# Both heads' causal masks of a peak block issued one behind the other

## The chip, the cores and the metric

The kernel runs on one core of one Trainium2 chip. The time is the device time of one execution, in microseconds (us), as the median of several runs. TensorE is PE in the profile, and its weight loads are PEld; VectorE is DVE, ScalarE is ACT, GpSimd is POOL, and SyncE is SP.

## The reference

One inference step of a two-layer trunk: a chunked gMLP layer, then a forgetting-attention layer with 16 heads of width 64, over a prompt of 1024 positions and 8 decoded samples. The part that matters here is the attention of the prompt (abridged):

```python
logits = jnp.einsum('nqhd,nkhd->nhqk', q, k).astype(jnp.float32) * (FA_HEAD_DIM ** -0.5)
decay = jnp.swapaxes(c_q, 1, 2)[..., :, None] - jnp.swapaxes(c_k, 1, 2)[..., None, :]
causal = k_pos[None, :] <= q_pos[:, None]
logits = jnp.where(causal, logits + decay, -jnp.inf)
p = jax.nn.softmax(logits, axis=-1)
return jnp.einsum('nhqk,nkhd->nqhd', p.astype(v.dtype), v)
```

A softmax wants the largest logit of each query row before its exponentials. All heads are computed, and all products are f32 in effect: the large ones are three passes over a split of both operands into a high and a low part.

## The kernel before, in words

The gMLP layer fills the first 990 us or so. The attention layer follows in eight phases `phase(j)`, each for one pair of heads, j = 0 to 7; phases 1 to 6 are one hardware loop. Phases 0 to 6 last 81.7 us each. In each of them TensorE, in an order written out by hand, does two things by turns:

- `step(j + 1, q, n)`: 64 pieces of three 512-column matmuls (the helper `three`, L1669 to L1671) that project keys, queries, values and gates of the next pair of heads. `steps(a, b)` issues pieces a to b.
- the attention of the pair j: `peak`, `spread`, `scores` and `values`.

Phase 7 has no next pair. Its `steps` are empty, and what stood between the attention's parts is gone.

`peak(j, qt)` finds the largest logit for the 128 queries of block qt, for both heads. For each head TensorE multiplies the queries with the keys 0 to (qt + 1) * 128 (L1944: one matmul for qt 0 to 3, two for qt 4 to 7, the second with 128, 256, 384 or 512 columns; f32 with 4-byte weights). Then it adds the causal mask to the last 128 columns by a matmul of a bf16 mask with a bf16 identity (L1945), which signals `m_done` once per head. DVE's `peak` waits for `m_done` of a head, then reduces that head's block to one number a row (L1381, one custom instruction and a read of its accumulator into `nmin`) and signals `nl_ready`.

The blocks live in PSUM. For qt under 4, both heads of a block share a pair of banks, and two pairs alternate. For qt from 4, head 0 always has `pair(2)` and head 1 `pair(1)`. So head h of block qt can be written only when DVE has reduced head h of block qt - 1, and TensorE waits for it on `nl_ready`:

```python
if qt == 4:
    pe.wait_ge(S("nl_ready"), 16 * j + 8) if h == 0 else pe.wait_ge(S("mb_ready"), 2 * j + 1)
if qt > 4:
    pe.wait_ge(S("nl_ready"), 16 * j + 2 * qt + h - 1)
```

For qt 4, head 1 waits for `mb_ready`: `spread(j, 0)` (L1955) has put the first half's row numbers into `pair(1)`, and ACT's `shift` copies them out (L888). `peak_round` on DVE rounds the numbers of four blocks (L1387) ahead of each `spread`. After block 7, `scores(j, 0)` (L1974, L1975) writes to head 1's pair and waits for DVE's last reduction. From the scores the work goes to DVE (`exponents`, L1420), ACT (`probs`, L897 and L899), POOL (`p_low`, L524) and back to TensorE (`values`, L1993 to L1995).

In phases 0 to 6, blocks 0 and 1 stand together behind six pieces of steps, blocks 2 and 3 together behind three more, and each of the blocks 4 to 7 has three or four pieces between itself and what comes next. In phase 7 the blocks 4 to 7 and `scores(7, 0)` follow one another with nothing between. After phase 7's first scores, POOL sends for the samples' queries (`load_q`, tile `qb`), DVE scores the paged cache (L1364, L1367) between its other work, and the output projection and the sample's tail end the kernel.

Of the kernel before, what the change touches and what calls it, by code (L numbers as in the profile page):

```python
# [59 lines left out]
def wait(eng, sem, value):  # L60

    if isinstance(value, int) and value <= 0:
        return
    eng.wait_ge(sem, value)
# [7 lines left out]
def trunk(nc, units, w_ada0, w_ada, c_t, x_t, cols_d, ws_t, bs_row, ln_rows, table, cache_k, cache_v, cache_f,  # L72
          y_out, ys_out, k_out, v_out, f_out, kqv_s_out, vn_out):
    ctx = ExitStack()
    with ctx:
        sems = {}

        def S(name):
            if name not in sems:
                sems[name] = ctx.enter_context(nc.semaphore(name))  # L80
            return sems[name]
# [14 lines left out]
        def const(name, shape, dt=F32):  # L96
            n = 1
            for s in shape[1:]:
                n *= s
            t = at(name, shape, dt, const_end[0])  # L100
            const_end[0] += (n * (2 if dt == BF16 else 4) + 31) // 32 * 32
            assert const_end[0] <= 229368
            return t
# [88 lines left out]
        identb = const("identb", [P, P], BF16)  # L192
        ones = const("ones", [P, P])
        maskb = const("maskb", [P, P], BF16)
# [69 lines left out]
        def pair(n):  # L264
            return ps[n][:, :, :].rearrange("p a b -> p (a b)")
# [14 lines left out]
        def peak_out(qt, h):  # L280

            return ps[1 + qt % 2][:, h, 0:(qt + 1) * P] if qt < 4 else pair(2 - h)[:, 0:(qt + 1) * P]
# [1381 lines left out]
        def _(pe):  # L1664
            mm = nc.tensor.matmul
# [260 lines left out]
            def peak(j, qt):  # L1926

                qs = slice(qt * P, (qt + 1) * P)
                if qt == 0:
                    pe.wait_ge(S("kq_lo"), 4 * j + 4)  # L1930
                    wait(pe, S("arg_ready"), 24 * j)
                if qt == 1:
                    pe.wait_ge(S("v_hl"), j + 1)
                if 2 <= qt < 4:
                    pe.wait_ge(S("nl_ready"), 16 * j + 2 * qt - 2)
                for h in range(2):
# [4 lines that stand above are left out]
                    out = peak_out(qt, h)  # L1941
                    for k in range(0, (qt + 1) * P, HALF):
                        ks = slice(k, min(k + HALF, (qt + 1) * P))
                        mm(out[:, ks], QA[:, h, qs], KA[:, h, ks], start=True, stop=ks.stop < (qt + 1) * P)  # L1944
                    mm(out[:, qs], maskb[:, :], identb[:, :], start=False, stop=True).then_inc(S("m_done"), 1)  # L1945

            def spread(j, half):

# [68 lines left out]
            def phase(j, more):  # L2017
# [5 lines left out]

                steps(0, 6)
                peak(j, 0)
                peak(j, 1)
                if not more:
                    pe.wait_ge(S("ev_s"), 4 * KB)
                    pe.wait_ge(S("zs_done"), 4 * KB)
                    turn(1, 0)  # L2030
                steps(6, 9)
                peak(j, 2)
                peak(j, 3)
                steps(9, 13)
# [56 lines left out]
            for b in range(KB):  # L2091
# [18 lines left out]
                if b == 6:  # L2110
# [7 lines left out]
                    for c in range(2):  # L2118
                        last = mm(bank(6)[:, c:c + 1], ex[:, c, :, :].rearrange("p b h -> p (b h)"), ones[0:NS, 0:1],
                                  start=True, stop=True)  # L2120
# [19 lines left out]
            for n in range(NS):  # L2140
                s, (odd, p) = n % 4, divmod(n, NP)
                pe.wait_ge(S(f"pages_in{s}"), 16 * NP * (n // 4 + (5 if s < 2 else 1)))
                for h in range(2):
                    for g in range(4):
                        rows = slice(2 * H * g, 2 * H * (g + 1))
                        last = mm(bank(6 + h)[rows, :], PZ[:, p, 2 * g + odd, :], pages[:, s, g, h * 512:(h + 1) * 512],
                                  start=False, stop=n == NS - 1)
# [105 lines left out]
```

## Time and profile before

| | |
|---|---|
| median of 3 runs (lowest, highest) | 1831.62 us (1830.38, 1832.17) |
| the profiled execution, its span | 1832.32 us, 1830.7 us |
| PE busy | 1683.2 us (92%) |
| DVE busy | 996.8 us (54%) |
| ACT busy, POOL busy | 623.6 us (34%), 426.5 us (23%) |
| one phase (1160.0 to 1241.7) | PE 80.3 of 81.7 us |

How to read it: the busy times are shares of the whole span, and a matmul counts from its start to a modelled end, so consecutive matmuls overlap in the records. What a matmul costs is better read as the distance from its start to the start of the next one, and so it is done here ("distance"). Times are from the start of the span.

### The profile page before, as it was taken

The numbers are of one execution on the slowest core, as the hardware profiler recorded it, in microseconds if no ns is written. First come the engines' busy times: TensorE is split into PE (matmuls) and PEld (weight loads), VectorE is DVE, ScalarE is ACT, GpSimd is POOL, SyncE is SP. The second block draws the span as 40 slices with busy tenths as digits, with TensorE's granted clock in tenths as the row PEclk, the third lists the DMA queues.
The fourth block names the chain that finished last, engine by engine and source line by source line (L and its number), as shares of the span: only waits on it lengthen the run. The fifth ranks groups of instructions, "written<-read, shape, count | busy, mean of one in ns | idle before, by whom it ended". The sixth has DMA issues, their size and how long they took to land.

```text
span 1830.7 us, 28121 instructions
## 1 busy us (share of the span) xinstructions
PE 1683.2 (92%) x10192; PEld 1463.2 (80%) x10192; DVE 996.8 (54%) x1552; ACT 623.6 (34%) x980; POOL 426.5 (23%) x432
## 2 busy tenths in 40 slices
PE   6999999999999979999679999999999999759985
PEld 4899999999999969999567778787777778447742
DVE  3423353434343463245534676766767776789775
ACT  2311221111111153235322546463644546252121
POOL 0000011101110100002210526253443526354221
PEclk9999999999999999999889999999999999669987
DMA  8111121222122203234222221212112120418757
GB/s 348 35 46 46 34 91 60 92 82 80 67 92 80 82 23 116 92 119 146 69 73 70 81 59 58 85 48 85 46 69 69 57 79 35 141 36 274 247 231 299
DMA packets 50191, 180.45 MB, mean 99 GB/s; under 512 B 6522, under 2 KB 8186, under 8 KB 48850
## 3 DMA queue, kind: packets, MB, share of 16 engines
q1 hardware_dynamic: 31650, 116.11, 18.7%
q0 software_dynamic: 18480, 63.53, 9.7%
q8 instruction: 38, 0.62, 0.1%
q14 instruction: 23, 0.19, 0.0%
HBM read 154.07 MB, written 17.15 MB: 94 GB/s over the span
## 4 chain that ended last, share of the span: by engine, by line
PE 76%; DVE 10%; issue 4%; ACT 4%; POOL 2%; DMA 2%; POOLq 0%; DVEq 0%; SPq 0%; ACTq 0%
PE bank L1669 20%; PE bank L1671 18%; PE bank L1670 18%; PE bank L1944 2%; PE bank L1993 2%; PE bank L1801 2%; POOL p_lo L524 2%; PE bank L1975 2%; PE bank L1974 2%; PE bank L1995 2%; PE bank L1994 2%; DVE pages L1364 1%; DMA fsw<-units 1%; PE bank L1781 1%; DVE scol L1367 1%
## 5 line engine op out<-in xcount | busy, mean ns | idle before, releaser
L1669 PE MATMUL bank<-h_hi,w_lo 128*128 128x344 f32 x1152 | 373.8, 325 | 8.1 <-DVE h_lo L1052 8.0
L1670 PE MATMUL bank<-h_lo,w_hi 128*128 128x344 f32 x1152 | 367.9, 319 | 0.0
L1671 PE MATMUL bank<-h_hi,w_hi 128*128 128x344 f32 x1152 | 367.7, 319 | 0.0
L524 POOL TENSOR_TENSOR p_lo<-parg,p_hi 128x512 fp32r<-128x512 f32 (+1 forms) x192 | 220.6, 1165 | 178.9 <-ACT p_hi L899 177.7
L1669 PE MATMUL bank<-x_hi,w_lo 128*128 128x512 f32 x528 | 223.8, 424 | 11.3 <-POOL x_lo L481 6.4
L1669 PEld LDWEIGHTS bank<-h_hi,w_lo 128*128 128x128 f32 x1152 | 217.0, 188 | 13.4 <-issue 9.2
L1670 PEld LDWEIGHTS bank<-h_lo,w_hi 128*128 128x128 f32 x1152 | 217.1, 188 | 0.2 <-issue 0.2
L1671 PEld LDWEIGHTS bank<-h_hi,w_hi 128*128 128x128 f32 x1152 | 216.8, 188 | 0.0
L1670 PE MATMUL bank<-x_lo,w_hi 128*128 128x512 f32 x528 | 211.4, 400 | 0.0
L1671 PE MATMUL bank<-x_hi,w_hi 128*128 128x512 f32 x528 | 211.4, 400 | 0.0
L1669 PE MATMUL bank<-y_hi,w_lo 128*128 128x320 f32 (+2 forms) x512 | 179.5, 351 | 25.7 <-ACT y_hi L720 9.4
L1010 DVE TENSOR_TENSOR w_lo<-raw,w_hi 128x1024 fp32r<-128x1024 f32 x105 | 151.1, 1439 | 75.0 <-ACT w_hi L645 73.1
L1670 PE MATMUL bank<-y_lo,w_hi 128*128 128x320 f32 (+2 forms) x512 | 176.4, 344 | 0.0
L1671 PE MATMUL bank<-y_hi,w_hi 128*128 128x320 f32 (+2 forms) x512 | 175.9, 344 | 0.0
L1420 DVE SCALAR_TENSOR_TENSOR parg<-bank,cph,mb 128x512 f32<-128x512 f32 (+1 forms) x192 | 109.0, 608 | 98.7 <-PE bank L1975 97.4
L463 POOL TENSOR_TENSOR vcur<-V,vr 128x1024 f32<-128x1024 f32 x16 | 30.7, 1921 | 522.2 <-PE bank L1801 319.0
L897 ACT ACTIVATE parg<-parg 128x512 f32<-128x512 f32 (+1 forms) x192 | 98.9, 515 | 139.2 <-DVE parg L1420 139.0
L645 ACT ACTIVATE w_hi<-raw 128x1024 fp32r<-128x1024 f32 x105 | 111.2, 1059 | 60.0 <-PE bank L1671 53.7
L1669 PEld LDWEIGHTS bank<-x_hi,w_lo 128*128 128x128 f32 x528 | 102.3, 194 | 34.9 <-POOL x_lo L481 6.8
L1669 PEld LDWEIGHTS bank<-y_hi,w_lo 128*128 128x128 f32 x512 | 98.9, 193 | 36.9 <-issue 24.7
L1381 DVE CUSTOM_DVE_ANT_0 bank<-bank,ckb 128x256 f32<-128x256 f32 (+7 forms) x128 | 94.6, 781 | 48.0 <-PE bank L1945 46.9
L1671 PEld LDWEIGHTS bank<-x_hi,w_hi 128*128 128x128 f32 x528 | 101.2, 192 | 24.2
(298 smaller groups left out, 2680.2 us busy)
## 6 DMA issues: line engine op xcount, KB each, us to landing
raw<-units SPq DMA_DIRECT2D x121, 512.0 KB, 3.4
ada_ring<-w_ada SPq DMA_DIRECT2D x32, 512.0 KB, 3.3
pages<-cache_k POOLq DMA_DIRECT2D x32, 512.0 KB, 5.5
pages<-cache_v POOLq DMA_DIRECT2D x32, 512.0 KB, 7.4
ada_first<-w_ada SPq DMA_DIRECT2D x8, 1024.0 KB, 14.9
ckb<-scr_c POOLq DMA_DIRECT2D x16, 512.0 KB, 4.4
KX<-KA SPq DMA_DIRECT2D x32, 256.0 KB, 4.2
xT<-x_t SPq DMA_DIRECT2D x2, 2064.0 KB, 23.3
```

Source lines behind the costliest of these rows:

```text
L524: g.tensor_tensor(p_lo[:, r, off:HALF], parg[:, r, off:HALF], p_hi[:, r, off:HALF].bitcast(F32), ALU.subtract).then_inc(S("p_ready"), 1)
L645: A(w_hi[:, slot, :, :], raw[:, slot, :, :], ACT.Copy).then_inc(S("hi_ready"), 1)
L897: A(parg[:, r, off:HALF], parg[:, r, off:HALF], ACT.Exp, scale=SCALE).then_inc(S("p_exp"), 1)
L1010: v.tensor_tensor(w_lo[:, slot, :, :], raw[:, slot, :, :], w_hi[:, slot, :, :].bitcast(F32), ALU.subtract)\
L1381: v.tensor_tensor_reduce(out=out, in0=out, in1=ckb[:, h, 0:(qt + 1) * P], scale=-1.0, scalar=3e38, op0=ALU.add, op1=ALU.min, accum_out=nmi ...
L1420: v.scalar_tensor_tensor(parg[:, r, off:HALF], ps[1 + slot][:, h, off:HALF], cph[:, h, kt:kt + 1], mb[:, h, off:HALF], ALU.add, ALU.add).t ...
L1669: mm(out, lhs_lo, rhs_hi, start=first, stop=False)
L1670: mm(out, lhs_hi, rhs_lo, start=False, stop=False)
L1671: return mm(out, lhs_hi, rhs_hi, start=False, stop=last)
L1801: last = mm(pair(3)[:, t * P:(t + 1) * P], vcur[:, t, :], rhs, start=True, stop=True)
L1944: mm(out[:, ks], QA[:, h, qs], KA[:, h, ks], start=True, stop=ks.stop < (qt + 1) * P)
L1974: mm(out, KA[:, h, ks], QA[:, h, qs], start=True, stop=False)
```

## The change

```diff
                     for k in range(0, (qt + 1) * P, HALF):
                         ks = slice(k, min(k + HALF, (qt + 1) * P))
                         mm(out[:, ks], QA[:, h, qs], KA[:, h, ks], start=True, stop=ks.stop < (qt + 1) * P)
-                    mm(out[:, qs], maskb[:, :], identb[:, :], start=False, stop=True).then_inc(S("m_done"), 1)
+                for h in range(2):
+                    mm(peak_out(qt, h)[:, qs], maskb[:, :], identb[:, :], start=False, stop=True).then_inc(S("m_done"), 1)
```

A block was: scores of head 0, mask of head 0, scores of head 1, mask of head 1. It is now: scores of head 0, scores of head 1, mask of head 0, mask of head 1. The waits of each head stay ahead of its own scores. The instructions are the same in number and form, in all 64 blocks of the eight phases. No other engine's program changes.

## Rows read from the trace of the kernel before

**Rows 1.** Busy time by stretch (stretch, its length, busy us of each engine, clock, DMA share, GB/s).
```profile
1160.00:1241.70 81.70, 80.30 (x449) 64.25 (x448) 58.30 (x100) 42.45 (x71) 34.08 (x31) 1.00 0.20 64
1573.70:1587.10 13.40, 10.86 (x32) 6.84 (x33) 10.48 (x19) 1.02 (x1) 1.03 (x2) 0.50 0.36 127
```

**Rows 2.** Timeline, PE, block 6 of phase 1 (start us, us, engine, line, out<-in).
```profile
1090.97 0.57 PE L1944 MATMUL bank<-KA,QA 128*128 128x512 f32 x2
1091.38 0.23 PE L1945 MATMUL bank<-identb,maskb 128*128 128x128 bf16 x1
1091.42 0.65 PE L1944 MATMUL bank<-KA,QA 128*128 128x512 f32 x2
1091.91 0.23 PE L1945 MATMUL bank<-identb,maskb 128*128 128x128 bf16 x1
1091.95 0.48 PE L1669 MATMUL bank<-x_hi,w_lo 128*128 128x512 f32 x1
1092.26 0.40 PE L1670 MATMUL bank<-x_lo,w_hi 128*128 128x512 f32 x1
```

**Rows 3.** Timeline, PE, block 0 of phase 1, its scores and the next block's.
```profile
1074.59 0.22 PE L1944 MATMUL bank<-KA,QA 128*128 128x128 f32 x1
...
1074.88 0.36 PE L1944 MATMUL bank<-KA,QA 128*128 128x256 f32 x1
```

**Rows 4.** Timeline, PE, narrow f32 matmuls behind one another.
```profile
1081.64 1.00 PE L1955 MATMUL bank<-identr,nminr 128*128 128x128 f32 x8
1082.49 0.45 PE L1669 MATMUL bank<-x_hi,w_lo 128*128 128x512 f32 x1
```

**Rows 5.** Timeline, PE, block 4 of phase 1.
```profile
1083.92 0.56 PE L1944 MATMUL bank<-KA,QA 128*128 128x512 f32 x2 [0.15 <-ACT mb L888]
1084.33 0.23 PE L1945 MATMUL bank<-identb,maskb 128*128 128x128 bf16 x1
```

**Rows 6.** Timeline, DVE, blocks 6 and 7 of phase 1.
```profile
1091.80 1.10 DVE L1381 CUSTOM_DVE_ANT_0 bank<-bank,ckb 128x896 f32<-128x896 f32 x1 [1.37 <-PE bank L1945]
...
1093.86 0.14 DVE L1381 DVE_READ_ACCUMULATOR2_ANT nmin<- 128x1 f32 x1
1095.01 1.23 DVE L1381 CUSTOM_DVE_ANT_0 bank<-bank,ckb 128x1024 f32<-128x1024 f32 x1 [0.93 <-PE bank L1945]
...
1097.35 0.14 DVE L1381 DVE_READ_ACCUMULATOR2_ANT nmin<- 128x1 f32 x1
```

**Rows 7.** Timeline, weight loads, the first of phase 1's scores.
```profile
1097.85 0.19 PEld L1974 LDWEIGHTS bank<-QA,KA 128*128 128x128 f32 x1
```

**Rows 8.** Timeline, DVE, blocks 4 and 5 of phase 7.
```profile
1578.12 0.83 DVE L1381 CUSTOM_DVE_ANT_0 bank<-bank,ckb 128x640 f32<-128x640 f32 x1 [0.59 <-PE bank L1945]
1578.87 0.14 DVE L1381 DVE_READ_ACCUMULATOR2_ANT nmin<- 128x1 f32 x1
1578.99 0.96 DVE L1381 CUSTOM_DVE_ANT_0 bank<-bank,ckb 128x768 f32<-128x768 f32 x1
```

**Rows 9.** Timeline, PE, blocks 4 to 7 and the first scores of phase 7.
```profile
1576.89 0.90 PE L1944 MATMUL bank<-KA,QA 128*128 128x512 f32 x2 [0.45 <-ACT mb L888]
1577.60 0.33 PE L1945 MATMUL bank<-identb,maskb 128*128 128x128 bf16 x1
...
1579.06 1.01 PE L1944 MATMUL bank<-KA,QA 128*128 128x512 f32 x2 [0.26 <-DVE nmin L1381]
1579.88 0.33 PE L1945 MATMUL bank<-identb,maskb 128*128 128x128 bf16 x1
...
1584.12 1.22 PE L1944 MATMUL bank<-KA,QA 128*128 128x512 f32 x2
1585.14 0.33 PE L1945 MATMUL bank<-identb,maskb 128*128 128x128 bf16 x1
1587.10 0.77 PE L1974 MATMUL bank<-QA,KA 128*128 128x512 f32 x1 [1.63 <-DVE nmin L1381]
```

**Rows 10.** The chain that ended last, behind phase 7's first scores (start, us, what).
```profile
1593.55 4.65 DMA qb<-scr_q
```

## The prediction, made before the changed kernel ran

> **What bounds the kernel now.** I read the page's engine shares first, then the busy time by stretch, then the start times of TensorE's instructions round a block, then DVE's, and last the chain that ended last.
>
> In a full phase TensorE is busy 80.3 of 81.7 us and DVE 58.3 [rows 1]. So in phases 0 to 6 the order of TensorE's own instructions sets the pace, and a saving there counts. The stretch of blocks 4 to 7 in phase 7 is different: TensorE is at the lower of its two levels (granted clock 0.50, 1.2 GHz), and TensorE and DVE are both busy for most of its 13.4 us [rows 1]. There the two take turns. TensorE waits for DVE's number before the scores (0.26 us at 1579.06), DVE waits for TensorE's mask (0.59 us at 1578.12), and 1.63 us pass before the first scores at 1587.10 [rows 8, 9]. Behind them the chain runs over exponentials and POOL to a transfer of the queries, which lasts 4.65 us and on which DVE's later work waits [rows 10].
>
> **What a mask costs.** Block 6 of phase 1 [rows 2]: head 0's scores take 0.41 us for 512 + 384 columns (1090.97 to 1091.38), the mask 0.04, head 1's same scores 0.49, the mask 0.04, and the next 512-column matmul 0.31. The f32 matmul behind a mask is 0.08 us dearer than the same work elsewhere: 0.49 against 0.41. I read this as the f32 weights that are loaded openly: the load can only begin when the mask starts. A mask with what follows it so costs 0.04 + 0.08 = 0.12 us, twice per block.
>
> **What the change removes and adds in a block.** Head 1's scores no longer follow a mask, and the two masks follow one another. So 0.12 us go, and a distance from mask to mask comes, which I call M. No row has two bf16 matmuls in a row. Its bounds:
> - Below, 0.04 us, the start-to-start distance of a mask and an f32 matmul [rows 2].
> - Above, 0.11 us, the distance of f32 matmuls of 128 columns: eight take 0.85 us [rows 4]. They pay an f32 load each.
> - I take 0.06, nearer to the lower end: 896 columns in 0.41 us are 0.06 for 128 columns, and the mask rows show that a mask's load adds nothing visible ahead of it.
>
> Blocks 1, 2, 3, 5, 6, 7: 0.12 - 0.06 = 0.06 us gained each, 0.36 together. Block 0: head 0's scores are 128 columns, too short to hide an f32 load, so head 1's come 0.11 us behind its own load instead. Its four matmuls take 0.29 us now (1074.59 to 1074.88) [rows 3], and then 0.06 + 0.11 + 0.06 + 0.04 = 0.27: 0.02 gained. Block 4: head 1's scores start at 1083.92, when ACT's copy is done, whatever stood before them [rows 5]. The mask of head 0 now lies inside that wait and is free; behind the wait it costs M: 0.06 lost. Sum in TensorE's own work: 0.36 + 0.02 - 0.06 = 0.32 us a phase.
>
> The Trainium skill speaks against this. Its page "TensorE: Matmul & The Clock Gate", section "Back-to-back issue gap", gives about 81 ns a matmul for a sustained stream of weight load and 128-column matmul. By that, as an estimate, M would be 0.08, the six blocks would gain 0.04 each and the phase about 0.18 us before any wait. No row of this case shows the pair; the rows show 0.04 for a lone mask and 0.11 for f32.
>
> **What the change delays.** Head 0's mask now stands behind head 1's scores and behind head 1's wait. DVE starts 0.42 us after the mask's start (1091.38 to 1091.80) [rows 2, 6], and it reduces both heads without a pause, so its whole pair is later by head 1's scores less what was saved.
> - Blocks 0 and 1: DVE is behind anyway. Blocks 2 and 3: later by 0.17 us; four pieces of steps stand between them and `spread`, nothing is lost. Block 4: 0.8 us later, 3.3 us before head 0's scores of block 5 come. Block 5: 0.35 later, with 0.4 to spare at block 6.
> - Block 6: DVE's last number is done at 1094.00 [rows 6], and 0.41 later by the change. Head 1's scores of block 7 want to load their weights at about 1094.39. They get them at 1094.45, and with the load less well hidden I count 0.04 us.
> - Block 7: DVE ends at 1097.49 now [rows 6], and 0.45 later, at 1097.94. The first scores load at 1097.85 now [rows 7], and would at 1097.77. They wait for the signal (1097.98) and the open load (0.11): 0.09 to 0.19 us late, I take 0.13. Everything behind (exponentials, POOL, `values`) is timed from these scores.
>
> A phase gains 0.32 - 0.04 - 0.13 = 0.15 us; seven phases 1.05 us. M stands once in each of the eight blocks. With M = 0.04 they give 0.16 more, less 0.07 of longer waits: 0.24 a phase; with no wait at block 7 and the scores at all it would be 0.40, or 2.8 us in seven phases. With M = 0.11 they give 0.40 less, and the waits fall by 0.10: -0.15 a phase, -1.05 us.
>
> **Phase 7.** Nothing stands between the blocks here. Head 0's mask used to be ready while DVE was still on the block before. Now DVE must wait until head 1's scores, which themselves wait for DVE's last number, are through. Durations at this level: scores with an open load 0.71 us (640 columns), 0.82 (768), 0.92 (896, between its neighbours), 1.02 (1024) [rows 9]; from mask to DVE 0.51 (1577.60 to 1578.12) [rows 8, 9]; a reduction until its number is out 0.89, 1.03, 1.16, 1.29, in steps of 0.13 from 1578.12 to 1579.01 and 0.96 + 0.07 for 768 [rows 8]; from the number to TensorE 0.04 to 0.05 (1579.01 to 1579.06).
> - Block 4: head 0's mask goes from before the wait to 1577.60. DVE starts at 1578.11; its first number is out at 1579.00, its second at 1579.79 instead of 1579.01.
> - Block 5: 1579.00 + 0.04 + 2 x 0.82 + 0.51 + 1.03 = 1582.22 for the first number.
> - Block 6: + 0.04 + 2 x 0.92 + 0.51 + 1.16 = 1585.77.
> - Block 7: + 0.04 + 2 x 1.02 + 0.51 + 1.29 = 1589.65, and the second number 1.25 later, 1590.90.
>
> It comes at 1586.95 now (0.14 us ahead of the scores at 1587.10 [rows 9]), so phase 7 loses 3.95 us. Before it, blocks 0 and 1 give about 0.12 us to the samples' matmuls that follow them (two opened loads less, one mask-to-mask more, at the lower level), and block 2 puts DVE 0.17 us back, as in every phase, but with nothing to hide it. Loss 4.0 us. Bounds: 3.3 (a weight load better hidden in three blocks, 0.18 each, and shorter signals) to 4.6. I see no cover: POOL's query transfer waits for the last number too, and DVE's backlog after it is in order.
>
> **Sum.** -1.05 + 4.0 = +2.95 us on the profiled 1832.32, so 1835.3. That execution lies 0.7 above the median of the runs, 1831.62; on the median it makes 1834.5. About 0.2%, 3.7 us, is what a measurement of this kernel can tell from no change (so below 1827.9 or above 1835.3). The forecast is a small loss inside it.
>
> **Rivals.**
> - Slower: mask behind mask costs like a narrow f32 matmul, M = 0.11, from the first pair on. The loops then lose 1.05 us and phase 7 4.0 to 4.6: 1836.7 to 1837.3. For it: no row shows the pair, and a load that can't hide under another mask's short stream is what the f32 rows pay. Against: no load is exposed ahead of the lone masks [rows 2]. It decides from M = 0.09 on.
> - Faster or even: the phases' gain arrives as computed and phase 7's lateness is swallowed behind it, say by the query transfer or by the cache transfers of the tail. Then -1.05 to -2.8: 1828.8 to 1830.6. For it: the tail is partly paced by transfers. Against: the transfer at 1593.55 is issued only after the last number [rows 10], so it moves along.
> - The clock: phase 7 and the stretch behind it change their level. If some 3 us of blocks 4 to 7 ran at 2.4 GHz, two scores of about 0.9 us would halve and the loss would shrink by 1 us (1833.5); if more idle time holds the lower level longer behind them, 1 to 2 us come on top, 1835.5 to 1836.5. For it: the stretch has the 0.50 level with TensorE busy 10.9 of 13.4 us [rows 1].
> - The change doesn't remove what I say: the 0.08 us behind a mask stays with head 1's scores for another reason. Then the phases lose 0.5 us each, 1839. Only against it: the same scores cost 0.41 where an f32 matmul is ahead.
>
> **Chances.** Forecast 0.52 (1832.5 to 1836, of which 0.08 is over the bound), slower by M 0.20, swallowed 0.12, clock 0.13, not removed 0.03. Slower by over 0.2%: 0.08 + 0.18 + 0.05 + 0.03 = 0.34. Faster by over 0.2% needs the swallowed case with most of its gain and an end beyond it: 0.07. The same: 0.59. The range takes both ends of M, phase 7's bounds and a microsecond of clock: 1830.6 to 1837.8.
>
> **What would show it.** Right: in block 6 of a phase, head 1's scores take 0.41 us and two masks stand about 0.06 apart; a phase is 81.5 to 81.6 us long; in phase 7 DVE waits 1.3 us or more for the mask before each of blocks 5, 6 and 7, and the first scores start about 4 us later against the phase's start. Wrong: masks 0.1 us apart, phases longer than 81.7, no new idle time of TensorE before the first scores, or phase 7's scores late by under 3 us.

## The result, and the profile after

Changed: 1832.97 us median of 20 runs, against 1831.22 us for the kernel before (20 runs). The medians are 1.75 us apart. The ratio of the runs, which is not that of the two medians, is 1.0016 (2.9 us), 95% interval 1.0009 to 1.0023, which is 1.6 to 4.2 us slower. The forecast was 2.95 us slower. The profiled execution took 1836.33 us (span 1834.7), 4.0 us more than the one before.

Block 6 of phase 1 after, the timeline of TensorE, answers to [rows 2]:

```profile
1090.97 0.98 PE L1944 MATMUL bank<-KA,QA 128*128 128x512 f32 x4
1091.79 0.29 PE L1946 MATMUL bank<-identb,maskb 128*128 128x128 bf16 x2
1091.89 0.47 PE L1669 MATMUL bank<-x_hi,w_lo 128*128 128x512 f32 x1
1092.20 0.39 PE L1670 MATMUL bank<-x_lo,w_hi 128*128 128x512 f32 x1
```

Both heads' scores now take 0.82 us, twice 0.41; the 0.08 us that head 1's scores paid behind head 0's mask are gone. The second mask by itself:

```profile
1091.86 0.22 PE L1946 MATMUL bank<-identb,maskb 128*128 128x128 bf16 x1
```

It starts 0.07 us behind the first, and the next matmul 0.03 behind it. The two masks take 0.10 us together, where a lone one took 0.04: the second mask adds 0.06. The next f32 matmul still pays its 0.31. From the first scores to L1670 the block takes 1.23 us, and took 1.29 [rows 2].

Block 7 of the same phase, TensorE's timeline:

```profile
1094.06 1.14 PE L1944 MATMUL bank<-KA,QA 128*128 128x512 f32 x4
1095.04 0.28 PE L1946 MATMUL bank<-identb,maskb 128*128 128x128 bf16 x2
```

The scores of 1024 columns each take 0.98 us for both heads. Head 0's alone took 0.47 in the kernel before, so this is 0.04 to 0.05 more than twice that. I read it as head 1's weight load, which comes open behind DVE's number of block 6.

DVE in blocks 6 and 7 of the same phase, and the weight load and matmul of the first scores, from the timeline; they answer to [rows 6, 7]:

```profile
1092.21 1.10 DVE L1381 CUSTOM_DVE_ANT_0 bank<-bank,ckb 128x896 f32<-128x896 f32 x1 [1.37 <-PE bank L1946]
...
1095.46 1.23 DVE L1381 CUSTOM_DVE_ANT_0 bank<-bank,ckb 128x1024 f32<-128x1024 f32 x1 [0.96 <-PE bank L1946]
...
1097.80 0.14 DVE L1381 DVE_READ_ACCUMULATOR2_ANT nmin<- 128x1 f32 x1
1097.99 0.19 PEld L1975 LDWEIGHTS bank<-QA,KA 128*128 128x128 f32 x1 [0.25 <-DVE nmin L1381]
1098.01 0.48 PE L1975 MATMUL bank<-QA,KA 128*128 128x512 f32 x1
1098.33 0.40 PE L1976 MATMUL bank<-QA,KX 128*128 128x512 f32 x1
```

DVE's last number is out at 1097.94, and the weight load, which used to run ahead with no wait, now has a wait of 0.25 us for it. The matmul starts in time and then takes 0.32 us instead of 0.23, 0.09 us lost. I put it down to the late weight load.

Phase 7 after, the timeline of TensorE, answers to [rows 9]; below it DVE's first reductions of each block, which answer to [rows 8]:

```profile
1576.73 0.90 PE L1944 MATMUL bank<-KA,QA 128*128 128x512 f32 x2 [0.58 <-ACT mb L888]
1577.43 0.44 PE L1946 MATMUL bank<-identb,maskb 128*128 128x128 bf16 x2
1578.90 1.79 PE L1944 MATMUL bank<-KA,QA 128*128 128x512 f32 x4 [1.03 <-DVE nmin L1381]
1580.49 0.44 PE L1946 MATMUL bank<-identb,maskb 128*128 128x128 bf16 x2
1582.09 2.03 PE L1944 MATMUL bank<-KA,QA 128*128 128x512 f32 x4 [1.16 <-DVE nmin L1381]
1583.93 0.44 PE L1946 MATMUL bank<-identb,maskb 128*128 128x128 bf16 x2
1585.66 2.27 PE L1944 MATMUL bank<-KA,QA 128*128 128x512 f32 x4 [1.30 <-DVE nmin L1381]
1587.73 0.44 PE L1946 MATMUL bank<-identb,maskb 128*128 128x128 bf16 x2
1590.87 0.77 PE L1975 MATMUL bank<-QA,KA 128*128 128x512 f32 x1 [2.70 <-DVE nmin L1381]
```

```profile
1577.95 0.83 DVE L1381 CUSTOM_DVE_ANT_0 bank<-bank,ckb 128x640 f32<-128x640 f32 x1 [2.77 <-PE bank L1946]
...
1581.01 0.97 DVE L1381 CUSTOM_DVE_ANT_0 bank<-bank,ckb 128x768 f32<-128x768 f32 x1 [1.39 <-PE bank L1946]
...
1584.45 1.10 DVE L1381 CUSTOM_DVE_ANT_0 bank<-bank,ckb 128x896 f32<-128x896 f32 x1 [1.49 <-PE bank L1946]
...
1588.25 1.23 DVE L1381 CUSTOM_DVE_ANT_0 bank<-bank,ckb 128x1024 f32<-128x1024 f32 x1 [1.60 <-PE bank L1946]
```

Here the two engines take strict turns. TensorE idles 1.0 to 1.3 us for the number, does both heads' scores and masks, and only then DVE, idle for 1.4 to 1.6 us, has something to do.

The same two stretches by busy time, answering to [rows 1]:

```profile
1156.29:1237.79 81.50, 80.02 (x449) 64.30 (x448) 58.43 (x100) 42.44 (x71) 34.06 (x31) 1.00 0.20 64
1573.54:1590.87 17.33, 10.56 (x32) 6.45 (x33) 10.05 (x19) 1.02 (x1) 0.54 (x1) 0.50 0.25 88
```

**Where the 4.0 us of the two profiled executions are.** Cut at the first scores of each phase's block 0, at phase 7's `spread` and at its first attention scores (start times of TensorE's timeline; the differences are of unrounded times):

| stretch | before | after | difference |
|---|---|---|---|
| up to phase 0's first block | 993.55 | 993.90 | +0.36 |
| phases 0 to 6, to phase 7's first block | 569.00 | 567.82 | -1.19 |
| phase 7, first block to `spread` | 11.15 | 11.82 | +0.67 |
| phase 7, `spread` to first attention scores | 13.40 | 17.33 | +3.93 |
| from there to the end | 243.64 | 243.87 | +0.23 |

The first and the last row are not the change's: over the eleven profiled executions of this study the first ran from 988.9 to 994.5 us and the last from 239.0 to 243.9, in no order that goes with the kernel. The runs of the changed kernel spread about as widely, from 1828.0 to 1837.8. The third row is dealt with below.

### The profile page after: what moved, and what is told of

The parts are those of the page before. It is cut to its first block, busy times and chain, and to the rows that moved or that the text cites. A ratio compares the mean times of both kernels' runs of the same rounds, so it can differ in the third digit from the quotient of the medians.

```text
span 1834.7 us, 28121 instructions
## 1 busy us (share of the span) xinstructions
PE 1680.9 (92%) x10192; PEld 1463.8 (80%) x10192; DVE 996.8 (54%) x1552; ACT 623.3 (34%) x980; POOL 426.5 (23%) x432
## 4 chain that ended last, share of the span: by engine, by line
PE 76%; DVE 10%; issue 4%; ACT 4%; DMA 2%; POOL 2%; POOLq 1%; DVEq 0%; SPq 0%; ACTq 0%
PE bank L1669 20%; PE bank L1671 18%; PE bank L1670 18%; PE bank L1944 2%; PE bank L1994 2%; PE bank L1801 2%; POOL p_lo L524 2%; PE bank L1975 2%; PE bank L1976 2%; PE bank L1996 2%; PE bank L1995 2%; DVE pages L1364 1%; DMA fsw<-units 1%; PE bank L1781 1%; DVE scol L1367 1%
## 5 line engine op out<-in xcount | busy, mean ns | idle before, releaser
L1669 PE MATMUL bank<-h_hi,w_lo 128*128 128x344 f32 x1152 | 374.7, 325 | 8.9 <-DVE h_lo L1052 8.9
L1670 PE MATMUL bank<-h_lo,w_hi 128*128 128x344 f32 x1152 | 368.8, 320 | 0.0
L1669 PE MATMUL bank<-x_hi,w_lo 128*128 128x512 f32 x528 | 223.3, 423 | 11.3 <-POOL x_lo L481 6.4
L1669 PEld LDWEIGHTS bank<-h_hi,w_lo 128*128 128x128 f32 x1152 | 217.8, 189 | 13.7 <-issue 10.9
L1670 PEld LDWEIGHTS bank<-h_lo,w_hi 128*128 128x128 f32 x1152 | 217.8, 189 | 0.2 <-issue 0.2
L1670 PE MATMUL bank<-x_lo,w_hi 128*128 128x512 f32 x528 | 211.0, 400 | 0.0
L1669 PE MATMUL bank<-y_hi,w_lo 128*128 128x320 f32 (+2 forms) x512 | 179.7, 351 | 26.0 <-ACT y_hi L720 9.3
L1670 PE MATMUL bank<-y_lo,w_hi 128*128 128x320 f32 (+2 forms) x512 | 176.1, 344 | 0.0
L1669 PEld LDWEIGHTS bank<-x_hi,w_lo 128*128 128x128 f32 x528 | 101.5, 192 | 34.9 <-POOL x_lo L481 6.8
L1669 PEld LDWEIGHTS bank<-y_hi,w_lo 128*128 128x128 f32 x512 | 99.0, 193 | 37.3 <-issue 24.7
```

Of the source, the lines that this page charges most:

```text
L1669: mm(out, lhs_lo, rhs_hi, start=first, stop=False)
L1670: mm(out, lhs_hi, rhs_lo, start=False, stop=False)
```

## The experiments

All stretches are cut as in the table. "Phases of" gives the shortest and longest distance from one phase's first block to the next one's, for the phases 1 to 5; phase 0 and phase 6 are shorter to the next start (81.05 and 79.47 us before). Before, phases 1 to 5 took 81.68 to 81.71 us. All kernels but the two with fp32r masks keep the bf16 masks; the function was written so that a condition chooses the order block by block:

```diff
-                    mm(out[:, qs], maskb[:, :], identb[:, :], start=False, stop=True).then_inc(S("m_done"), 1)
+                    if not paired:
+                        if h == 0 and early_wait:
+                            head_wait(1)
+                        mask(h)
+                if paired:
+                    mask(0)
+                    mask(1)
```

where `mask(h)` is the old line for head h and `head_wait(h)` the head's old wait, which stands ahead of its scores as before.

**The changed order in phases 0 to 6 only**, `paired = not last_phase`:

> The changed order in phases 0 to 6 only; phase 7 keeps the old order. My theory (the phases gain, phase 7 alone loses): each phase 81.50 to 81.55 us as with the whole change, phase 7 from its spread to its first scores 13.4 us as before, time 1.2 us below the kernel before (1830.0 on a median of 1831.2, ratio 0.9993). Rival (the later reductions cost something in the phases too, or the gain is swallowed by the start of phase 7): time equal to before, 1831.2.

Measured: phases of 81.46 to 81.53 us, `spread` to scores 13.40. The time is 1829.78 against 1830.28, ratio 0.9998 (0.9990 to 1.0007), so the runs can't tell it from before; the gain of 1.4 us (567.64 against 569.00 us for phases 0 to 6) shows only in the cut of the profiled execution. The phases keep their gain without phase 7's loss.

**The changed order in phase 7 only**, `paired = last_phase`:

> The changed order in phase 7 only. My theory: phases 81.69 us as before, from phase 7's spread to its first scores 17.3 us instead of 13.4, and the time 3 to 4 us over before where TensorE's clock is at its lower level there: 1834.2 to 1835.2 (ratio 1.0016 to 1.0022). Rival (part of the lateness is swallowed behind it by the query transfer or in the tail): the scores 3.9 us late, but the time only 1.5 to 2.5 us over before.

Measured: phases of 81.67 to 81.70 us, 17.32 from `spread` to scores, 1833.95 us, ratio 1.0019 (1.0009 to 1.0029): 3.7 us over before by the medians, 1.6 to 5.3 by the interval. That fits all of the lateness arriving at the end, but the rival that had part of it swallowed is not excluded by the times: its 1.5 us are just outside the interval, its 2.5 inside. The traces narrow it. POOL's first query transfer is issued 6.45 us behind phase 7's first scores before and with this change, and the last one 122.3 us behind them before and 122.5 here. So nothing is swallowed in the first 122 us. For the rest, whose end varies by more than the effect, it is not shown.

**The wait alone**, `early_wait = last_phase and qt >= 4`, nothing paired:

> The old order of masks everywhere, but in blocks 4 to 7 of phase 7 the wait of head 1 stands ahead of head 0's mask. It tells what of phase 7's loss is the wait and what is head 1's scores ahead of the mask. My theory (it is the scores): worked out with the durations of the prediction, the first scores come 0.5 us later than before, from spread to scores 13.9 us, time within 0.03% of before plus 0.5: 1831.7. Rival (a mask behind head 1's wait is what costs, however short the rest): 2 us or more, spread to scores 15.4 or above, time 1833.2.

Measured: 13.84 us, 0.44 more than before, ratio 1.0003 (0.9995 to 1.0012). A part of its blocks 4 and 5, TensorE's timeline:

```profile
1576.88 0.29 PE L1943 MATMUL bank<-identb,maskb 128*128 128x128 bf16 x1 [0.58 <-ACT mb L888]
1576.93 0.88 PE L1954 MATMUL bank<-KA,QA 128*128 128x512 f32 x2
...
1578.31 1.01 PE L1954 MATMUL bank<-KA,QA 128*128 128x512 f32 x2 [0.36 <-DVE nmin L1381]
1579.12 0.33 PE L1943 MATMUL bank<-identb,maskb 128*128 128x128 bf16 x1
1579.21 0.99 PE L1954 MATMUL bank<-KA,QA 128*128 128x512 f32 x2
```

Head 0's mask (L1943) waits for the same signal as with the change, but head 1's scores run after it, beside DVE. So of phase 7's 3.93 us the wait alone is worth 0.44, and the rest comes only when head 1's scores stand ahead of the mask too.

**Phase 7 cut further.** `paired = last_phase and qt > 4`, and `paired = last_phase and qt == 4`, one execution each, which is the profiled one:

> The changed order in blocks 5, 6 and 7 of phase 7 only. Worked out with the prediction's durations: block 4's numbers come as before, block 5's first number 1.4 us later than before, and then the two engines take strict turns (wait, head 1's scores, mask, DVE) for three blocks: the first scores 3.1 us late, spread to scores 16.5 us. Rival (each block gives its own share of the 3.9 us, a quarter or so): 2.9 us would be 16.3; rival (block 4 opens the gap and the others only keep it): 1 us or less, 14.4.

> The changed order in block 4 of phase 7 only. Worked out with the same durations: the pair of numbers of block 4 is 0.8 us late, and of that lateness blocks 5 to 7, in the old order, make 1.2 us at the first scores (DVE's head start over head 1 is used up once): spread to scores 14.6 us. Rival (DVE catches up in the idle times it has in blocks 5 to 7): 13.4 to 13.8.

Measured: 16.53 and 14.58 us, 3.14 and 1.18 more than before. Both are the sums worked out beforehand. (The times were 1834.48 and 1831.97 us against 1831.17, too few to say more.) Together they make 4.3, not 3.93, so the shares do not add. With blocks 5 to 7 paired, pairing block 4 as well adds 0.80 us, which is the lateness of block 4's second number in the prediction (1579.79 for 1579.01); where blocks 5 to 7 keep the old order, the same pairing of block 4 costs 1.18.

**Which blocks to pair.** `paired = not last_phase and qt not in (4, 7)`:

> The changed order in phases 0 to 6 for blocks 0 to 3, 5 and 6; the old order for blocks 4 and 7 there and for all of phase 7. My theory: block 4 gives back the 0.07 us that mask behind mask costs behind ACT's wait, and block 7 gives up 0.05 but the first scores need not wait for DVE (0.09): a phase 81.42 to 81.45 us, time 1.8 to 1.9 us below before (1829.4, ratio 0.9990). Rival (the waits at block 7 and at the scores cost nothing, so leaving block 7 out only loses its gain): 81.50 us a phase, no better than the changed order in all blocks of these phases.

Measured: phases of 81.35 to 81.38 us, 1827.09 against 1830.28, ratio 0.9981 (0.9971 to 0.9991). It beats the kernel before, and the changed one lies on the other side of that. A little more was won in the phases than I had worked out, 0.34 us each where I had 0.26. Phases 0 to 6 together are 2.35 us shorter (566.65 us); the medians differ by 3.2. The interval, 1.6 to 5.3 us, holds both, and the larger figure is not shown to be the order's. And with block 7 paired too, `paired = not last_phase and qt != 4`:

> The changed order in phases 0 to 6 for all blocks but block 4, the old order in phase 7. With the changed order in every block a phase took 81.46 to 81.53 us, without blocks 4 and 7 81.35 to 81.38. It splits the 0.12 us between the two. My theory: 0.06 to 0.07 belong to block 4 (mask behind mask lies behind ACT's wait), the rest, 0.05, to block 7 and the first scores' wait: a phase 81.42 to 81.44, time about 1.8 us below before. Rival (block 7's wait is all of it, block 4 nothing): 81.48 or more. Rival (block 4 is all of it): 81.37 or less.

Measured: phases of 81.42 to 81.46 us, ratio 0.9983 (0.9971 to 0.9994). So block 4's pairing costs 0.05 to 0.06 of the 0.12 us, and block 7's 0.07 to 0.08. The rows of the changed kernel account for block 7: the pairing wins 0.06 in TensorE's work and gives back 0.14 behind DVE's numbers, 0.05 in its own scores and 0.09 in the first scores of the attention. Block 4 in the mix, TensorE's timeline:

```profile
1083.88 0.23 PE L1943 MATMUL bank<-identb,maskb 128*128 128x128 bf16 x1
1084.27 0.56 PE L1954 MATMUL bank<-KA,QA 128*128 128x512 f32 x2 [0.15 <-ACT mb L888]
1084.67 0.23 PE L1943 MATMUL bank<-identb,maskb 128*128 128x128 bf16 x1
1084.70 0.48 PE L1669 MATMUL bank<-x_hi,w_lo 128*128 128x512 f32 x1
```

Head 0's mask lies inside the wait for ACT and is free there. With the change it stood behind it, and from head 1's scores to the next piece of steps (L1669) it was 0.50 us (1083.93 to 1084.43) where it is 0.43 here and was 0.45 before.

**What the open 0.08 us is.** TensorE's weight loads in block 6 of phase 1 of the kernel before:

```profile
1091.38 0.31 PEld L1944 LDWEIGHTS bank<-KA,QA 128*128 128x128 f32 x2
...
1091.91 0.20 PEld L1669 LDWEIGHTS bank<-x_hi,w_lo 128*128 128x128 f32 x1
```

Both begin with the mask ahead of them (1091.38 and 1091.91 in [rows 2]). The masks as fp32r, in the old order (the diff is shortened; POOL makes an f32 mask, DVE rounds it, and DVE's own masking of the scores reads it with 4 bytes too):

```diff
-        identb = const("identb", [P, P], BF16)
-        maskb = const("maskb", [P, P], BF16)
+        maskf = const("maskf", [P, P])
+        maskb = at("maskb", [P, P], F32R, const_end[0] - 512)
...
-                    mm(out[:, qs], maskb[:, :], identb[:, :], start=False, stop=True).then_inc(S("m_done"), 1)
+                    mm(out[:, qs], maskb[:, :], identr[:, :], start=False, stop=True).then_inc(S("m_done"), 1)
```

> The old order, with the masks as 4-byte (fp32r) matmuls of mask and identity in place of bf16 ones. It asks what the 0.08 us behind a mask is. My theory: an f32 weight load of some 0.11 us that starts with the matmul ahead of it and finds only 128 columns, 0.06 us, to hide behind; the type of the mask has no part in it. Then the f32 mask's own load is hidden by the scores and the cost is the same: scores of head 1 plus mask in block 6 still about 0.12 us over 0.41, a phase 81.65 to 81.75 us, time as before. Rival (it is a switch of the array between bf16 and f32): no switch, so the 0.08 us go behind every mask: 64 x 2 x 0.08 less, a phase 81.0 us or less, over 4 us faster.

and with these masks the changed order in phases 0 to 6:

> The same fp32r masks, and the changed order in phases 0 to 6 only. My theory: mask behind mask now costs an f32 load, 0.11 us, and so the pairing gains nothing: about 0.01 us a block is won and the waits of DVE's later numbers (up to 0.1 us a phase) stay: a phase 0.00 to 0.12 us longer than with the fp32r masks in the old order. Rival (the pairing saves by the order as such, whatever the type): a phase 0.2 us shorter than with the fp32r masks in the old order, as with bf16.

Block 6 of phase 1, TensorE's timeline, first in the old order, then paired:

```profile
1091.13 0.57 PE L1944 MATMUL bank<-KA,QA 128*128 128x512 f32 x2
1091.54 0.22 PE L1945 MATMUL bank<-identr,maskb 128*128 128x128 f32 x1
1091.60 0.62 PE L1944 MATMUL bank<-KA,QA 128*128 128x512 f32 x2
1092.06 0.22 PE L1945 MATMUL bank<-identr,maskb 128*128 128x128 f32 x1
1092.12 0.44 PE L1669 MATMUL bank<-x_hi,w_lo 128*128 128x512 f32 x1
1092.40 0.39 PE L1670 MATMUL bank<-x_lo,w_hi 128*128 128x512 f32 x1
```

```profile
1089.80 0.98 PE L1954 MATMUL bank<-KA,QA 128*128 128x512 f32 x4
1090.62 0.33 PE L1943 MATMUL bank<-identr,maskb 128*128 128x128 f32 x2
1090.79 0.45 PE L1669 MATMUL bank<-x_hi,w_lo 128*128 128x512 f32 x1
1091.08 0.39 PE L1670 MATMUL bank<-x_lo,w_hi 128*128 128x512 f32 x1
```

In the old order an fp32r mask takes 0.06 us and what follows it 0.05 more than elsewhere (0.46 against 0.41): 0.11 in all, where the bf16 mask took 0.12. The type of a lone mask hardly matters. What follows pays some 0.11 us from the mask's start in both, which is what a load of 0.11 us that starts with the mask would give. The phases took 81.63 to 81.65 us, ratio 0.9990 (0.9979 to 1.0001). The rival of a switch between types, which wanted 81.0 us, falls. Paired, the two masks take 0.17 us, 0.11 from one to the other, and the block 1.28 against 1.27. The pairing wins nothing in this block then. The phases took 81.77 to 81.85 us, 0.14 to 0.21 longer, all over the 0.00 to 0.12 that I expected; ratio 1.0003 (0.9993 to 1.0013). What I had left out is block 4: there the mask of head 0 moves from inside ACT's wait to behind it, and from head 1's scores to L1669 it was 0.50 us in the old order (1084.08 to 1084.58) and 0.62 paired (1082.64 to 1083.26). So the pairing pays here because the second bf16 mask adds 0.06 us; a second fp32r one adds 0.11.

## Why the prediction was right, step by step

- **M, mask behind mask.** Taken at 0.06 between 0.04 and 0.11. Measured: the masks start 0.07 apart, the matmul behind them follows 0.01 sooner than behind a lone mask, and so the second mask adds 0.06 (two masks 0.10, a lone one 0.04). The rival with M = 0.11 is what the fp32r masks do, not the bf16 ones. The 0.08 of the Trainium skill's "Back-to-back issue gap" ("TensorE: Matmul & The Clock Gate") is above what these rows show; they are pairs and no sustained stream. The 0.18 us a phase that the prediction worked out from it should have been 0.16 by its own count, since M stands once in each of the eight blocks.
- **The blocks.** 0.06 us gained in block 6 and 0.02 in block 0 (0.27 us where it took 0.29), as said. Block 4's loss, said to be 0.06, is 0.05 in the rows and 0.05 to 0.06 between the two mixes.
- **The waits in the phases.** Head 1's scores of block 7 lose 0.04 to 0.05 us (0.04 said), the first scores 0.09 (0.13 said).
- **A phase.** Said 0.15 us gained, seven 1.05. Measured 1.19 in the profile after and 1.36 with the change in phases 0 to 6 only; the waits, taken some 0.03 too high, are part of the difference.
- **Phase 7, blocks 4 to 7.** Said 3.95, measured 3.93 (3.92 with the change in phase 7 alone). So close a match is partly luck: both heads' scores of block 5 took 1.59 us where 1.64 was taken, those of block 7 2.07 for 2.04. Both mechanisms, the wait and head 1's scores ahead of the mask, are separated by the experiments above; the said sum didn't separate them.
- **No cover behind it.** Right as far as the traces go, 122 us behind the first scores; the time fits it (3.7 us with the change in phase 7 only, 1.6 to 5.3 by the interval) but would also fit a loss of some of it in the tail.
- **Phase 7, blocks 0 to 3.** I had +0.05 there. With the changed order in phase 7 only it is that: 11.20 us against 11.15. The profile of the whole change shows +0.67, and the clock is the difference between the two. Blocks 2 and 3, by busy time (stretch, its length, busy us of each engine, clock, DMA share, GB/s), in the kernel before and after:

```profile
1568.60:1572.00 3.40, 1.69 (x8) 0.98 (x8) 3.40 (x12) 0.00 (x0) 1.08 (x2) 1.00 0.49 183
1568.50:1572.00 3.50, 2.45 (x8) 1.35 (x8) 2.82 (x14) 0.00 (x0) 1.51 (x3) 0.50 0.35 109
```

  Before, TensorE had the 2.4 GHz level (granted clock 1.00) there, having been busy 5.63 of the 6.05 us ahead of it; after, it stayed at 0.50, having been busy 5.11 of 6.78, and the first scores of block 2 took 0.49 us where they took 0.29. In all six profiled executions with the old order in phases 0 to 6 the level rose in this stretch, and the stretch took 11.09 to 11.20 us. In the five with a changed order in those phases it took 10.63 to 11.82, and in two of them, the whole change and the bf16 change in all blocks of phases 0 to 6 (11.69), the level did not rise. That is one execution of each kernel. It suggests that the order in the phases shifts the clock in phase 7's start, a side effect that no term of the prediction has; whether it does, or chance, stays open.
- **The sum.** Said 2.95 us slower, measured 1.75 by the medians and 2.9 by the ratio (1.6 to 4.2 by its interval). The cut without blocks 0 to 3 and without the ends gives 2.74. The match of the ratio to 0.1 us is luck, as the interval is 2.6 us wide and the ends vary by 5; what is shown is the cut, term by term. I have no profile of a run at the median to say where the rest is.

## What to carry to other kernels

Before moving an instruction that signals another engine, ask what now runs ahead of the signal, in the stretch where nothing covers it: the same edit won some 0.17 us in each of seven phases that TensorE paces, and lost 3.9 us in the one phase where TensorE and DVE take turns. Pair short matmuls where one behind the other is cheap (here 0.06 us in bf16, against 0.11 in fp32r, which won nothing), so that only the last of them leaves an open load in front of a dear one; leave a short one alone where it lies inside a wait. And choose block by block: phases 0 to 6 gained 1.2 to 1.4 us with every block paired and 2.35 with blocks 4 and 7 left out, and phase 7 is best left as it was.

## What the runs showed of the hardware that was not expected

- An fp32r mask is no dearer than a bf16 one as long as it stands alone: 0.11 against 0.12 us with what it does to its follower. Each phase was even 0.05 us shorter with it.
- The eleven profiled executions, one of each kernel, differ by up to 5.6 us ahead of phase 0 (988.9 to 994.5), where the program is the same but for how the masks are made, and by 4.8 behind phase 7's first scores (239.0 to 243.9), more than the whole effect. The phases 1 to 5 repeat to within 0.1 us where the order in them is the same. A change this small is read from the phases.
